# Two stretches of unread TensorE products in each mixer replaced by projections from the groups behind them

## What is computed

```python
for l in range(DEPTH):                      # 2 layers
    h = rms_norm(x, ln_mix_pre[l])
    z = h @ w_in[l]
    z_q, z_kv, z_g, z_ret, z_rwkv, z_conv, z_gate = split_cols(z, IN_SIZES)
    o_nsa = nsa_mixer(z_q..., z_kv, z_g, ...)          # sparse attention
    o_ret = retention_mixer(r_q, r_k, r_v, r_g, ...)   # rotary, decay, head norm
    o_rwkv = rwkv7_mixer(z_rwkv, ...)                  # token shift, LoRA, recurrence
    o_conv = short_conv_mixer(z_conv, conv_w[l])
    gates = jax.nn.sigmoid(z_gate).reshape(B, S, N_BRANCHES, D_MODEL)
    merged = sum over m of gates[:, :, m] * (branches[m] @ w_branch[l, m])
    x = x + rms_norm(merged @ w_mix_out[l], ln_mix_post[l])
    ...                                     # cross attention, MLP
```

## Time and profile before

| what | value |
|---|---|
| median of 3 runs | 2041.87 us (2037.39 to 2044.82) |
| profiled execution, first to last instruction (span) | 2041.5 us; the page gives no other time for it |
| TensorE busy | 1951.0 us, 96% |
| VectorE busy | 1423.1 us, 70% |
| ScalarE busy | 1168.1 us, 57% |
| products of constants, 128x256, without reader | 320 rows (two for each product), 78.8 us |
| chain that ended last, by engine | PE 64%, DVE 23%, ACT 8% |

### The profile page before, as it was taken

One profiled execution on the slowest core, in us unless ns is written; L12 is line 12 of the kernel. 1 busy time (PEld: TensorE's weight loads), 2 busy tenths in 40 slices (PEclk: granted clock), 3 DMA queues, 4 the chain that ended last, 5 costly groups with the idle time before them and its releaser, 6 DMA issues.

```text
span 2041.5 us, 29505 instructions
## 1 busy us (share of the span) xinstructions
PE 1951.0 (96%) x12546; PEld 1747.7 (86%) x12546; DVE 1423.1 (70%) x1424; ACT 1168.1 (57%) x1310; POOL 76.5 (4%) x94
## 2 busy tenths in 40 slices
PE   7999999999999999999999999999889999999997
PEld 6989998988998989999887999887778888888875
DVE  4586648546555677647745555757679999999996
ACT  4544344555444554334654444465388888888884
POOL 0000013000000000004000000000000000000000
PEclk9999999999999999999999999999999999999999
DMA  7333365534554443346544555433369999999993
GB/s 283 140 126 132 122 250 199 207 124 160 191 186 146 160 145 135 130 157 262 206 145 154 191 186 186 143 116 124 124 254 379 375 379 376 376 375 377 374 390 155
DMA packets 64520, 440.80 MB, mean 216 GB/s; under 512 B 7372, under 2 KB 7372, under 8 KB 14592
## 3 DMA queue, kind: packets, MB, share of 16 engines
q1 hardware_dynamic: 55296, 399.63, 52.4%
q0 software_dynamic: 8096, 35.30, 4.7%
q10 hardware_dynamic: 992, 3.93, 0.5%
HBM read 428.61 MB, written 10.23 MB: 215 GB/s over the span
## 4 chain that ended last, share of the span: by engine, by line
PE 64%; DVE 23%; ACT 8%; issue 2%; POOL 1%; DMA 1%; DVEq 0%; ACTq 0%; POOLq 0%
PE psum L188 63%; DVE ring_low L202 7%; ACT hl L198 4%; DVE arena L212 3%; DVE ht L202 3%; DVE rounded L202 2%; DVE hl L202 2%; DVE rounded L212 2%; DVE arena L202 2%; POOL arena L202 1%; ACT arena L198 1%; PE psum L192 1%; DVE resid L202 1%; ACT rounded L198 1%; ACT gn L198 1%
## 5 line engine op out<-in xcount | busy, mean ns | idle before, releaser
L202 DVE TENSOR_TENSOR hl<-ring,hl 128x2048 fp32r<-128x2048 f32 (+1 forms) x190 | 433.6, 2286 | 306.1 <-ACT hl L198 305.7
L188 PE MATMUL psum<-ht,hl 128*128 128x256 f32 x4992 | 621.6, 285 | 5.7 <-DVE ht L202 5.7
L188 PEld LDWEIGHTS psum<-ht,hl 128*128 128x128 f32 x4992 | 607.6, 192 | 14.3 <-DVE ht L202 6.6
L198 ACT ACTIVATE hl<-ring 128x2048 fp32r<-128x2048 f32 (+1 forms) x286 | 536.3, 1896 | 111.3 <-PE psum L188 105.2
L198 ACT ACTIVATE arena<-psum 128x512 f32<-128x512 f32 (+5 forms) x232 | 120.9, 521 | 405.8 <-PE psum L188 374.7
L188 PE MATMUL psum<-hl,ax 128*128 128x512 f32 x1320 | 346.3, 392 | 2.0 <-ACT gn L198 1.2
L188 PEld LDWEIGHTS psum<-hl,ax 128*128 128x128 f32 x1320 | 246.7, 188 | 53.9 <-ACT gn L198 1.7
L202 DVE TENSOR_TENSOR ring_low<-ring,hl 128x2048 fp32r<-128x2048 f32 x96 | 215.4, 2286 | 20.5 <-ACT hl L198 20.3
L188 PE MATMUL psum<-arena 128*128 128x128 f32 (+6 forms) x1520 | 186.6, 288 | 4.2 <-ACT arena L198 2.4
L188 PEld LDWEIGHTS psum<-arena 128*128 128x128 f32 (+2 forms) x1520 | 172.2, 178 | 15.0 <-ACT arena L198 3.6
L188 PE MATMUL psum<-rounded 128*128 128x512 f32 (+2 forms) x640 | 132.4, 335 | 5.9 <-DVE par L202 3.2
(11 more groups left out here) (123 smaller groups left out, 2030.6 us busy)
## 6 DMA issues: line engine op xcount, KB each, us to landing
ring<-W SPq DMA_DIRECT2D x284, 1024.0 KB, 5.2
arena<-W SPq DMA_DIRECT2D x48, 1024.0 KB, 8.1
ht_raw<-W SPq DMA_DIRECT2D x46, 1024.0 KB, 7.8
gate_d<-arena POOLq DMA_DIRECT2D x32, 256.0 KB, 3.9
arena<-gate_d POOLq DMA_DIRECT2D x8, 1024.0 KB, 8.2
gn<-GB POOLq DMA_DIRECT2D x10, 512.0 KB, 4.3
arena<-GB POOLq DMA_DIRECT2D x6, 512.0 KB, 5.3
ring<-W SPq DMA_DIRECT2D x4, 512.0 KB, 5.2
```

The source lines that it names most:

```text
L188: return Nothing() if self.e is None else self.e.matmul(o, a, b, start=start, stop=stop, skip_group_check=skip_group_check)
L198: return self.e.activation(o, a, f, bias=bias, scale=scale)
L202: return Nothing() if self.e is None else self.e.tensor_tensor(o, a, b, op)
```

## The change

In `tensor` the two calls `warm(6)` of each layer become `fill()`. To keep the number of projections, the three behind the attention outputs become two, and of the two ahead of the `aPz` transposes one goes. Because the list of projections is worked off in order, each replaced call takes the next entry: `raw 0` now stands before the attention outputs, `bc 2` before the `rmean` sums, `u` before the `rvar` sums, and `gate 0` alone before the `aPz` transposes. The other engines' programs are the same. Each `fill()` takes a bank as `warm` did, so one bank less is taken in each of the two places.

```diff
--- before.py
+++ after.py
@@ -778,7 +778,7 @@
                     ins = pe.transpose(psum[:, b, 128 * t:128 * t + 128], flat(L.Sc[:, 4 * t:4 * t + 4, :]), C("ident"))
                 ins.then_inc(s_pe, P("pcT", l))
                 turn_p(2)
-                warm(6)
+                fill()
                 for j in range(2):
                     b = bank("onsa", j, l)
                     pe.wait_ge(s_act, A["pT", 2, 1, 1, l])
@@ -793,7 +793,7 @@
                 P.mark("nsa end", l)
 
 
-                fill(3)
+                fill(2)
                 pe.wait_ge(s_dve, V["lor", l])
                 for nm, rws in (("w2", slice(0, 32)), ("a2", slice(32, 64)), ("g2", slice(64, 128))):
                     b = bank(nm, l)
@@ -836,7 +836,6 @@
                 fill()
 
 
-                fill()
                 pe.wait_ge(s_dve, V["aPz", l])
                 for nm, src in (("v", L.v), ("b", L.bP), ("k", L.kP)):
                     b = bank("tm", nm, l)
```

## The result

| | before | after |
|---|---|---|
| median | 2042.9 us (2033.52 to 2045.33, 8 runs) | 2051.14 us (2050.36 to 2059.93, 8 runs) |
| ratio | | 1.0057, interval 1.0038 to 1.0076 |
| the same pair, measured again | 2038.06 us (12 runs) | 2053.98 us (6 runs), ratio 1.0087, interval 1.0063 to 1.0111 |
| profiled span | 2041.5 us | 2048.8 us |

The change makes the kernel slower by 0.57% in the first comparison and by 0.87% in the second. The ratios are not the quotients of the medians, which are 1.0040 and 1.0078 (8.2 and 15.9 us). Forecast were 2055 us, that is 13.4 us or 0.66% more; both intervals hold it. The time of an execution is its span and some 1.8 us (2050.62 us for the profiled one of after).

What follows compares the result with a forecast made beforehand. The prediction took waits on VectorE's and ScalarE's chains to decide in the mixer, despite TensorE's 96% busy. Per layer 2.78 + 1.05 + 1.1 + 1.75 = 6.7 us, twice 13.4 us: 2055 us, range 2045.5 to 2060.

Steps and rivals of the forecast that it cites:

- bank wait and fall: Before the sixth matrix M: TensorE waits 3.75 us for a late transpose bank, then a clock fall costs 1.75 us.
- the forecast's second edit: Behind `ro`: `bc 2` before `rmean`, `u` behind it, one projection fewer before `aPz`; net 1.05 us late per layer.
- The first edit: At the attention outputs: one projection ahead, two behind; outputs 2.78 us late, LoRA products after 6.4 us of idling.
- The price of the slow LoRA products: At the LoRA products: the clock's fall behind 6.4 us of idling costs 1.1 us per layer.
- The hint that the fall at `bonus` might go: At `bonus`: if the wait drops under 3 us, the clock's fall may go and give back 1.75 us.
- the row of 2.50 us without a fall: At 467.46: idling brought no fall; by it alone neither new wait costs, and the sum is 5.7 us smaller.
- rival 1: In both mixers: no new clock falls, the one at `bonus` stays; 7.7 us, 2049.5 us; chance 0.28 with its variant.
- Its variant, the fall at `bonus` gone: At `bonus`: no new clock falls and the existing one gone as well; 2046 us; chance within rival 1's 0.28.
- rival 4: Behind the LoRA wait: clock low over two falls, 3.5 us more slow time per layer, half lost; 2060 us; chance 0.10.
- rival 2: At the matrices M: banks do not bite, clock stays; 2.70 us gained, 2.78 lost; 2042 us, no change; chance 0.09.
- the removed products come straight off: At the LoRA products: TensorE is the bound, 4 x 2.7 = 10.8 us saved; 2031 us; chance 0.03.

Runs made afterwards that it cites:

- the first edit alone: Kernel before with only `raw 0` moved ahead of the attention outputs and two projections behind them; ratios 1.0049 (4 runs) and 1.0051 (7 runs).
- the refilled wait: Changed kernel with 14 unread products added between the two projections behind the attention outputs and the LoRA products; ratio 1.0059 (5 runs).
- the second edit alone: Kernel before with only `bc 2` ahead of `rmean`, `u` behind it, one projection ahead of the transposes; ratios 1.0086 (5 runs) and 1.003 (12 runs).

## Why the prediction was right

By its steps, per layer, in us:

| step | forecast | measured (layer 0) |
|---|---|---|
| `raw 0` before the attention outputs | +2.78 | 5.94 for 3.28: +2.66 |
| outputs to `bonus`: LoRA products at 1.2 GHz | +1.1 | 42.11 for 39.29: +2.82 |
| `bonus` to `ro`: fall of the clock | 0, perhaps -1.75 | 6.81 for 8.36: -1.55 |
| `ro` to the transposes | -2.70 | 20.82 for 23.42: -2.60 |
| transposes to U: bank wait and fall | +3.75 and +1.75 | 19.55 for 14.21: +5.34 |
| sum | +6.7 | +6.67 |

The 1.05 us of the forecast's second edit are the -2.70 of the fourth row and the 3.75 of the fifth.

The first edit went as forecast. The chain from the attention outputs to the LoRA products took 22.80 us in every profile, with whatever TensorE did in it: two projections, three, or two and fourteen unread products. It was covered before but for 0.59 us, so a projection moved out from behind its start could only lengthen the path. Shown by the first edit alone (+4.0 to +5.5 us per layer) and by the refilled wait.

The second edit went as forecast too: a wait for ScalarE at exactly the sixth matrix, which takes the bank of the first transpose. It starts 8.07 us behind the first matrix (157.41 to 165.48), where five matrices take 4.42: 3.65 us late, 3.75 forecast, some of it before the third matrix, as foreseen. The rest of the 5.34 is the fall, 1.69 us for 1.75. The wait appears with the second edit alone and goes when `rvar` comes before `u`.

One term was mis-sized, in two halves that cancelled, by luck. The price of the slow LoRA products was put at 1.1 us, since "part of the slow time lies in the longer wait". It cost 2.82: the clock stayed down for 10.2 us, not for the 3.4 us of the rows it was priced from, and nearly all work from the LoRA products to `rot` ran through it, while VectorE waited for the rotary sums (3.12 us of idle time, 0.28 before). The hint that the fall at `bonus` might go was left at zero in the sum; in the changed kernel it went in all four profiled layers, since TensorE was now late by more than VectorE and waited only 1.60 to 2.15 us there, and gave back 1.55. 2.82 - 1.55 = 1.27 against 1.1. That was not bound to happen: in layer 0 of the first edit's first profile the clock was back 6.3 us behind the LoRA products' start (9.1 in the changed kernel), `bonus` waited 2.97 us, and its fall came.

The rule that the prediction took from the Trainium skill ("TensorE: Matmul & The Clock Gate", "HAM oscillation"), that such a wait makes the work behind it start cold, holds here for every wait of 6.33 us. For the waits of 3.13 to 3.16 us at `bonus` it held in eight layers of eleven, and for the 2.91 us before the sixth matrix in all ten.

Two readings behind the clock's prices do not hold. The prediction counted on a fall at the sixth matrix because the wait would be 3.2 to 3.75 us, beyond 3.14; it was 2.91, and the fall came all the same. And the row of 2.50 us without a fall was one draw: in the second profile of the same kernel, behind the same 2.50 us, the clock was down from 469.3 on:

```profile
469.30:472.70 3.40, 3.40 (x10) 0.50 0.00 0
```

So it was weak evidence for rival 1. Also, only in layer 0 did the clock fall about half a us behind the restart of `bonus`; in layer 1 it was 1.3 us.

Of the rivals, the one without new falls of the clock would have given 3.83 us per layer; the falls were there in both profiles of the changed kernel. Its variant, the fall at `bonus` gone, did happen, together with the new falls. So did rival 4's mechanism, a longer stay at the lower clock behind the LoRA wait that makes VectorE's rotary step late: 2.82 is 1.7 more than the forecast's 1.1, and rival 4 had priced it as half of 3.5. Only because `bonus` gave back 1.55 us per layer did the sum come out at the forecast's, and not at rival 4's (2060; its own terms make 2059). That the banks would not bite (rival 2) failed by the 2.91 us before the sixth matrix. That the removed products come straight off failed at the place named: the wait at the LoRA products grew from 0.59 to 6.33 us.

Open: which execution gets which start. Over the twelve experiments' profiles and the two at hand it was 80.4 to 88.7 us; for four of the kernels profiled twice it repeated within 1.3 us, for the first edit it did not. Nothing here tells what sets it.

## What to carry to other kernels

When an engine at 96% waits even 0.6 us for another, find the chain that ends there, and ask where it starts: work moved from behind that start to ahead of it lengthens the path by its whole duration, and what it replaced turns into waiting. A useful step put in the place of idle filler also delays whatever hangs on the step behind it; here a sum of half a microsecond released a chain over two engines that frees PSUM banks 15 us later. Where filler covers no wait, delete it. Putting work into a wait that is there is worth trying too, but here it moved the wait more than it removed it, and alone it gave nothing in the times (1.0002).

## What was not expected of the hardware

- The clock's fall behind an idle time of the same length is not the same each time. After 6.33 us of idling TensorE was at 1.2 GHz for 10.2 or 13.7 us in all twelve profiled layers that had this wait. After 3.13 to 3.16 us at `bonus` it fell in eight layers (for 3.4 or 6.8 us), and in three it did not: from `bonus` to `ro` 8.3 to 9.4 us with, 6.8 without.
- Shorter waits can bring a fall too. Behind the 2.91 us before the sixth matrix it came in all ten layers. An idle time of 2.50 us stands ahead of the MLP of both layers in all 14 profiles; the clock fell within 1.5 us behind it in six of these 28 places. In layer 1 of the second edit's first profile it fell at 746.6 with no idle time over 0.9 us in the 30 us before.
- TensorE worked for 9 us at 1.2 GHz behind the LoRA wait (9.14 of 10.2 us busy) before the clock came back; behind the sixth matrix it was down for 3.4 us in eight layers and 6.8 in two.
- With `bc 0` ahead of `bonus` the clock fell at 137.4, 1.2 us behind the restart after the 2.11 us of idling before `ro`. Two other layers with this wait had no fall, so that the wait is its cause is not shown.
- The start of the kernel, the same instructions in every version, took 80.4 to 88.7 us. In the long ones either the clock was down for 10.2 us from 46, or the bias products waited 3.9 to 5.4 us for a DMA, with 6.8 us of 1.2 GHz around that wait. Times of one kernel spread over 10 to 15 us in sets of six runs and more. The start makes 8 us between profiles; how much it makes of the spread of the times is not shown. A change of 3 us needs the stretches of a profile and a dozen runs beside it.
